# Four chunks instead of three projected, attended and picked ahead of the rest in a hybrid decoder layer

## The reference, cut to what matters

```python
s = jnp.einsum('chpd,hpnd->chpn', q, sub_keys)
top_s, top_i = lax.top_k(s, K)
cand = top_s[:, :, 0, :, None] + top_s[:, :, 1, None, :]
best_s, best_j = lax.top_k(cand.reshape(C, Hh, K * K), K)
ia = jnp.take_along_axis(top_i[:, :, 0], best_j // K, axis=-1)
ib = jnp.take_along_axis(top_i[:, :, 1], best_j % K, axis=-1)
expert = ia * PEER_KEYS + ib
g = jax.nn.softmax(best_s, axis=-1)
a = jax.nn.gelu(jnp.einsum('cd,chkd->chk', xc, u_tab[expert]), approximate=False)
return jnp.einsum('chk,chkd->cd', g * a, v_tab[expert])
```

## Time and profile before

| | |
|---|---|
| median of 3 runs | 3838.88 us (3837.93 to 3848.43) |
| the profiled execution | 3854.53 us |
| its span, first to last instruction | 3852.7 us |
| DVE busy | 64% |
| PE busy, mean granted clock | 77%, 0.919 |
| POOL busy, ACT busy | 37%, 34% |
| DMA moved | 1297 MB, mean 337 GB/s |

### The profile page before, as it was taken

The page is one execution under the profiler, slowest core; times in us unless marked ns, Lnnn a source line. Parts: engine busy times, 40 slices in busy tenths (PEclk is TensorE's granted clock), DMA queues, the critical chain, the costliest instruction groups (busy, mean ns, idle before and its releaser), DMA issues.

```text
span 3852.7 us, 34961 instructions
## 1 busy us (share of the span) xinstructions
PE 2960.4 (77%) x8920; PEld 1531.1 (40%) x8920; DVE 2484.8 (64%) x5699; ACT 1298.7 (34%) x3333; POOL 1408.0 (37%) x1367
## 2 busy tenths in 40 slices
PE   8797967984886698889878887777778777765665
PEld 6655523431443355545434333333333333322222
DVE  0321217786776476656626888887877888788765
ACT  1212311221111244433324444443543444344333
POOL 0000003443675366556623333333333333333332
PEclk9997878997898699889989999999999999999999
DMA  7835145777998999888898999999999999999998
GB/s 291 267 133 197 56 203 197 239 269 266 350 348 316 340 343 339 326 308 305 333 362 329 404 410 415 415 407 421 401 409 418 414 408 409 419 407 415 419 412 349
DMA packets 274454, 1297.10 MB, mean 337 GB/s; under 512 B 27888, under 2 KB 63088, under 8 KB 180464
## 3 DMA queue, kind: packets, MB, share of 16 engines
q0 software_dynamic: 195120, 1073.83, 71.4%
q1 hardware_dynamic: 74384, 203.74, 14.2%
q10 hardware_dynamic: 4752, 17.30, 1.2%
HBM read 1231.07 MB, written 63.70 MB: 336 GB/s over the span
## 4 chain that ended last, share of the span: by engine, by line
DMA 31%; issue 8%; DVE 5%; PE 4%; ACT 3%; POOLq 0%; POOL 0%; DVEq 0%; SPq 0%; ACTq 0%
DMA s_ring<-peer_uv,s_expert 17%; DMA e_more_slots<-peer_uv,s_expert 10%; PE e_acc L503 2%; DVE e_part L427 1%; PE e_product L1860 1%; DMA e_more_slots<-peer_v,s_expert 1%; DMA s_scratch<-norm_final_row 1%; DMA next_h<-e_h 1%; DMA e_h<-norm_ffn_row 1%; DVE s_ring L394 1%; ACT L341 0%; ACT s_diagonal L324 0%; DVE e_top_at L1697 0%; DVE s_dots L394 0%; ACT s_gate L343 0%
## 5 line engine op out<-in xcount | busy, mean ns | idle before, releaser
L503 PE MATMUL e_acc<-s_ring,s_diagonal 128*128 128x512 f32 (+1 forms) x2168 | 899.3, 543 | 393.0 <-ACT s_diagonal L324 366.6
L394 DVE CUSTOM_DVE_ANT_0 s_ring<-s_ring,e_x_copy 128x1024 f32<-128x1024 f32 x548 | 667.5, 1218 | 223.4 <-DMA s_ring<-peer_uv,s_expert 215.5
L503 PEld LDWEIGHTS e_acc<-s_ring,s_diagonal 128*128 128x128 f32 x2168 | 396.0, 199 | 956.3 <-ACT s_diagonal L324 607.3
L278 POOL DMA_INDIRECT s_ring<-peer_uv,s_expert x462 | 438.2, 948 | 792.4 <-DVE e_part L427 558.3
L278 POOL DMA_INDIRECT s_ring<-peer_u,s_expert x331 | 383.9, 1160 | 475.6 <-DVE s_expert L1797 238.1
L503 PE MATMUL e_acc<-e_more_slots,s_diagonal 128*128 128x512 f32 (+1 forms) x948 | 375.9, 522 | 154.9 <-ACT s_diagonal L324 147.5
L278 POOL DMA_INDIRECT s_ring<-peer_v,s_expert x325 | 353.8, 1089 | 373.0 <-PE e_acc L503 100.3
L341 ACT ACTIVATE s_dots<-s_dots 128x1 f32<-128x1 f32 x704 | 142.2, 202 | 966.2 <-DVE s_dots L394 965.5
L324 ACT ACTIVATE s_diagonal<-s_ident,s_gate 128x128 f32<-128x128 f32 x949 | 371.0, 399 | 219.4 <-PE e_acc L503 99.9
L394 DVE CUSTOM_DVE_ANT_0 s_ring<-s_ring,s_x 128x1024 f32<-128x1024 f32 x245 | 299.4, 1222 | 109.1 <-DMA s_ring<-peer_u,s_expert 71.0
L278 POOL DMA_INDIRECT e_more_slots<-peer_uv,s_expert x231 | 217.5, 941 | 403.9 <-DVE e_part L427 273.5
(11 more groups left out here) (233 smaller groups left out, 3678.8 us busy)
## 6 DMA issues: line engine op xcount, KB each, us to landing
w_in_kept<-w_in SPq DMA_DIRECT2D x8, 1104.0 KB
w_in_gained<-w_in_kept SPq DMA_DIRECT2D x8, 1104.0 KB, 10.3
p_w_in<-w_in_gained SPq DMA_DIRECT2D x8, 1104.0 KB, 20.1
f_w_big<-w_mem_kv SPq DMA_DIRECT2D x4, 2048.0 KB, 19.2
f_w_big<-peer_w_q_t SPq DMA_DIRECT2D x2, 4096.0 KB, 17.9
peer_scores<-f_stage_s SPq DMA_DIRECT2D x16, 512.0 KB, 5.0
e_mem_scores<-mem_scores SPq DMA_DIRECT2D x2, 4096.0 KB, 14.8
e_mem_values<-mem_values SPq DMA_DIRECT2D x2, 4096.0 KB, 25.0
```

The source lines that it names most:

```text
L278: pool.indirect_dma_start(out=to, out_offset=None, in_=table, in_offset=bass.IndirectOffsetOnAxis(ap=self.expert[c % PICK_BUFFERS][:, k:k ...
L394: dve.tensor_tensor_reduce(row, row, x[:, :], 1.0, 0.0, ALU.mult, ALU.add, self.dots[:, k:k + 1]).then_inc(self.u_used, 1)
L503: last = pe.matmul(self.acc[:, at:to], self.diagonal[:, made % DIAGONALS, :], row[:, at:to], start=(n == group[0]), stop=(n == group[-1]))
```

## The change

One more chunk goes through A and B, one fewer through C, D and E. B holds 330 rows in place of 150, C holds 120 in place of 150, D 294 in place of 340, and E 1304 in place of 1408. The late parts of the four chunks in B lie between the rows 3, 70, 145, 285 and 330 (before: 3, 45, 100, 150). 52 picks that were gathered as pairs are gathered as two single rows each. In E the early part of the first chunk is spread over 146 rows (before 65), and its late part over the rows 894 to 1094. From row 894 on, rows, early parts and late parts are the same as before.

```diff
-PAIRS_FROM = 331
+PAIRS_FROM = 383
...
-FIRST = 3
-FIRST_CHOICES = [45, 100, 150]
-PICK_FIRST, PROJECT_REST, ATTEND_REST = 150, 300, 640
+FIRST = 4
+FIRST_CHOICES = [70, 145, 285, 330]
+PICK_FIRST, PROJECT_REST, ATTEND_REST = 330, 450, 744
 STAGES = [(PICK_FIRST, "pe", D), (PROJECT_REST, "split", 0), (ATTEND_REST, "split", BANK), (len(ROWS), "pe", 3 * D // 4)]
-FRONTS = [(ATTEND_REST, 705), (712, 894), (914, 1148), (1170, 1404), (1426, 1660)]
-CHOICES = [(705, 860), (894, 1094), (1150, 1350), (1406, 1606), (1662, 1862)]
+FRONTS = [(ATTEND_REST, 890), (914, 1148), (1170, 1404), (1426, 1660)]
+CHOICES = [(894, 1094), (1150, 1350), (1406, 1606), (1662, 1862)]
```

## The result

The changed kernel took 3876.7 us in the median of four runs (3874.1 to 3880.8), the kernel before 3838.4 us beside it (3837.3 to 3848.4): a ratio of 1.009, 95% interval 1.0073 to 1.0108. It is slower, by 38 us. The profiled execution took 3879.1 us, its span 3877.3 at a clock of 0.917.

A forecast was written before the change was run, and what follows sets the result against it. Transfers were taken to bound E, DVE's picking B. Terms 108 + 250 - 64 - 88 - 152 = +54 us on the 3838.9 median gave 3893 us (3860 to 3925); the range leaving out 2 in 10 was 3842 to 3940.

The forecast's parts named there:

- A: Stage that moves no rows: +108 us, 44.1 for projecting one more chunk and 64 (59 to 68) for attending.
- B: Stage where picking was said to set the pace: +250 us, to 686, for 180 more rows and one chunk's picking.
- C: Stage with projection beside rows: -64 us for one chunk and its 30 rows, chunk 0's end moving to B.
- D: Stage with attention beside rows: -88 us, its four-key-block part gone, the five-block part 97, the three others 10 more.
- E: Last stage, transfer-bound: -152 us; to row 894, start 74.4, 64 pairs 162, and 20 for early part and h, x transfers.
- transfers take over from DVE as the bound: B's third stretch, rows 145 to 285: 77 MB at single rows' 358 GB/s, 219 us against DVE's 178.
- The sign that I named: B's third stretch: DMA share over 0.93 and DVE waiting for `s_ring` would show transfers as the bound.
- Rival 3: The ring of 8 slots binds, not the DMA engines: third stretch of B 252 us, whole 3941 us; chance 0.16.
- Rival 1: Transfers bind nowhere before E: B + 202 with DVE setting the pace, E -160, whole 3814 us; chance 0.10.
- Rival 2: Same mechanism halfway: B's third stretch 195 us, D -100, whole about 3850 us, roughly even; chance 0.12.
- Rival 4: The extra picking is hidden in the fuller B as in E; given no chance of its own.
- The rule: 512 B suffices for line rate, so single rows could match pairs: B's third stretch 178 to 187, sum some 35 less.

The follow-up runs named there:

- before_again: The kernel before, unedited, run again for a second profile: 3830.3 us.
- half_gather: Changed kernel, gathers of rows 145 to 285 fetching 2 KB a partition in place of 4 KB, their number unchanged: that stretch took 212.2 us.
- half_issues: Changed kernel without the gathers of the 70 v rows in rows 145 to 285: that stretch took 191.0 us, the whole 3841.6 us.
- four_buffers: Changed kernel with a fifth buffer for chunk 0's picks and B's rows spread evenly: 3849.7 us, 1.0018 of before.
- after_again: The changed kernel, unedited, run again for a second profile: 3870.2 us, 1.0074 of before.
- dense_front: Changed kernel with E's first early part packed into 65 rows in place of 146: E to row 894 took 260.5 us.
- half_dot: Changed kernel, DVE reducing 512 of 1024 columns of each u row in rows 145 to 285: that stretch took 212 us.
- three_dense: The kernel before, still three chunks ahead, with 190 rows in B in place of 150: 3866.1 us, 1.0078 of before.

## Why the prediction was right, and where it was not

The time, 3876.7 us, lies in the range, and the forecast of 3893 is 16 us above it. Its exchange by stages holds: against before_again C, D and E give back 61 + 83 + 169 = 313 us for 180 rows, B takes 243 for them, and A asks 110 for none; the part behind row 894 took 9 more.

- **A: right.** +110 and +105 against 108. Projecting cost 44.1 us as read, which leaves some 60 to 65 for attending with four key blocks, inside the 59 to 68 asked for. The 0.7 us a head behind the 68 stands on no row.
- **B: the number right, the reason wrong.** 679.3 us against 686. That the number came out is in part luck. The stretches took 94, 132, 138, 215 and 101 where I had 93.5, 126, 137, 219 and 110.7, so three small misses cancel in part. The step that failed is "transfers take over from DVE as the bound", with single rows at 358 GB/s as their ceiling. 357 GB/s is what came out, but half_gather kept the time at half the bytes. What POOL's timeline shows instead is its issue of one gather in 1.25 us, 175 us for 140 rows, and 40 us in which the ring had no free slot; half_issues bears the first out up to 21 us. The earlier trace rows could have warned me: the plain chunk of C had 32 gathers, 38.9 of 54 us busy on POOL, which with 0.30 us between them are 48.5, and I read its 358 GB/s as the DMA engines' ceiling. Whether bytes or gathers hold it in C was not tried.
- **The sign that I named didn't tell the cases apart.** I asked for a DMA share over 0.93 and waits of DVE for `s_ring`. Both came, 0.96 and 41 us; but the waits are nearly as long with half the bytes. Rival 3 was to be known by POOL's waits for `e_acc` and `s_dots` with the DMA share low. Those waits came too, 34 us of them, at a high share. The cause is partly rival 3's, at the price of the forecast.
- **PE is in no sum of mine for B.** The earlier trace rows had it busy for 110.5 of 122.4 us in the second stretch, more than DVE's 96; I called DVE the bound there. half_issues and four_buffers point to PE as the next bound, at 185 of 191 and 136 of 145 us. In the second stretch of after PE has 130.4 of 137.5 us: its work grew by 20 us and the stretch by 15, so DVE's 12 and 2 for the DMA engines gave the right length for another reason.
- **C: right,** −61 (−67 with after_again's C) against −64, with no wait at L483 or L401 for the end of chunk 0 any more. The earlier trace rows had 10.8 us of them.
- **D: right as far as it can be told.** −83 and −98 (−78 and −94 with after_again's D), as D of before varies by 16. Its first part took 103 us, where I had 97, and the three others together 408, where the windows of the earlier trace rows have 417 and I had 10 more.
- **E: mis-sized by 11 to 15.** To row 894 it took 241.4 us, in after_again 245.0, not 256. Two terms were too large. The start "stays" at 74.4 us in the sum, but it took 66 us (68 in after_again). The 64 pairs took 175 us where 162 + 20 were forecast, so 13 of the 20 us were spent. With the early part packed as before, in dense_front, the start is 74.7 us again. So the 74.4 held a price of the packing, which the sum put down to the load of the tables.
- **From row 894: nearly the same.** It took 5 and 9 us more, 1 and 5 with after_again's 1516.2, where "not the same" was named as a sign of being wrong. DVE's busy time there is the same to 1 us; PE's is 1109 us at a clock of 0.95, before 1093 and 1085 at 0.97.
- **Rivals 1, 2 and 4.** Rival 1 failed in B, where the third stretch was not DVE's 178 us; in E its −160 was nearer than mine. Rival 2 wanted 195 us there, which the stretch reaches only with half of its gathers gone. Rival 4 was dropped because DVE was taken for the bound; half_dot shows that DVE had room in the third stretch, so part of the picking may have been hidden there. No run took the picking out.
- **The rule.** The third stretch did not shorten to 178 to 187 us. The Trainium skill, "DMA: Bandwidth & Descriptors", Specifications, gives 512 B as the least transfer for line rate. No run here refutes that, since bytes were not what held these rows. One gather of 0.524 MB in 1.25 us is 419 GB/s at most, before any gap, so this kernel's single rows can't show their own ceiling.

**What stays open:** why the slots come free late for 40 us when halving the work of DVE, of PE or of the DMA engines doesn't change it (halving DVE's and the DMA engines' together was not tried, and ACT's work, which makes the diagonals, was changed in no run); whether POOL's issue or the handling of the transfers behind it is what half the gathers relieve; why C grew in three_dense; and why the granted clock differs between the two profiles of D.

## What to carry to other kernels

Count the instructions that ask for transfers, and multiply by their closest spacing, before calling a stretch bound by bytes: a DMA share of 0.96 and an engine that waits for transfers both appeared here where half the bytes made no difference. Price a stretch by every engine that is over 80% busy in it, not by the one that the chain names. And where work is pulled ahead of its place, look for the buffer that forces the rows of one stretch together: here it was 20 us of a loss of 38, or of 29 in the comparison that had four_buffers in it.

## What the hardware showed

- In this kernel one indirect gather follows another on POOL after 1.25 us at the soonest, 0.94 of it busy, at 4 KB a partition. Pairs of 8 KB have the same busy time (0.945 us mean of 428), and half_gather's 143 gathers, 140 of them of 2 KB, took 138.2 us where the changed kernel's took 138.1. Between 2 and 8 KB the cost on POOL goes by the gather, not by the byte.
- The DMA share is not a share of peak bandwidth: 0.96 at 357 GB/s, 0.66 at 190. Half the bytes (47% less a second) took away a third of the busy share.
- The mean gather took POOL 154.80 / 120 = 1.29 us in C and 138.07 / 143 = 0.97 in the third stretch of B. No run looked for the reason.
